# Moving one third of the adaLN product from TensorE matmuls to GpSimd, in a one-core Trainium2 decoder block

## The reference, cut to what matters

```python
mod = jnp.dot(jax.nn.silu(c), w_ada[l]) + b_ada[l]          # c: (1, 1024), w_ada: (1024, 6144)
sh1, sc1, g1, sh2, sc2, g2 = jnp.split(mod[:, None, :], 6, axis=-1)
h = rmsnorm(x, norm1_g[l]) * (1.0 + sc1) + sh1
x = x + g1 * token_mixer(h, w_in[l], ..., w_merge[l])       # projection, attention, conv, gates, merge
h = rmsnorm(x, norm2_g[l]) * (1.0 + sc2) + sh2
x = x + g2 * moe(h, ...)                                    # top 4 of 32 experts
return rmsnorm(x, normf_g)                                  # x: (1, 256, 1024), one layer
```

## Time and profile before

| | |
|---|---|
| median of 3 runs | 1197.81 us |
| the profiled execution: its time, its span | 1198.26 us, 1196.5 us |
| TensorE busy, share of the span | 1157.0 us, 97% |
| VectorE, ScalarE, GpSimd busy | 413.8 us, 208.8 us, 19.9 us |
| HBM read | 469.08 MB, 393 GB/s over the span |
| mean granted TensorE clock | 0.998 |

### The profile page before, as it was taken

How to read it: one execution, slowest core, us unless ns; L and a number is a source line. 1 busy time by engine, 2 the same in 40 slices (tenths; PEclk the granted TensorE clock), 3 DMA queues, 4 the chain that set the end, 5 groups by cost and what they waited for, 6 DMA issues and landing times.

```text
span 1196.5 us, 15173 instructions
## 1 busy us (share of the span) xinstructions
PE 1157.0 (97%) x6133; PEld 524.9 (44%) x6133; DVE 413.8 (35%) x792; ACT 208.8 (17%) x331; POOL 19.9 (2%) x38
## 2 busy tenths in 40 slices
PE   7999999999999999999999999999999999999997
PEld 4787899984333333333333333333333333333332
DVE  4667776663232322222222222222222322222222
ACT  4346644341011010101010101010101101010001
POOL 1000010000000000000000000000000000000000
PEclk9999999999999999999999999999999999999999
DMA  9998457699999999999999999999999999999995
GB/s 337 393 374 326 170 188 245 245 393 368 428 422 431 428 432 427 437 426 434 431 428 433 426 437 427 426 427 428 429 436 425 436 428 432 432 427 435 422 426 234
DMA packets 53171, 470.55 MB, mean 393 GB/s; under 512 B 4479, under 2 KB 10060, under 8 KB 31894
## 3 DMA queue, kind: packets, MB, share of 16 engines
q1 hardware_dynamic: 50884, 467.99, 94.1%
q10 hardware_dynamic: 2258, 2.16, 0.6%
HBM read 469.08 MB, written 1.06 MB: 393 GB/s over the span
## 4 chain that ended last, share of the span: by engine, by line
PE 71%; DMA 24%; ACT 2%; SPq 1%; DVE 1%; issue 1%; DVEq 0%; ACTq 0%
PE ps L1104 25%; DMA expert<-in_w_down 17%; PE ps L1114 15%; PE ps L875 14%; DMA expert<-in_w_gate_up 6%; PE ps L1080 4%; PE ps L1052 3%; PE ps L1033 2%; PE ps L819 1%; PE ps L1060 1%; ACT r_cu L1358 1%; DMA ada_first<-in_w_ada 1%; PE ps L732 1%; SPq L489 1%; PE ps L1096 1%
## 5 line engine op out<-in xcount | busy, mean ns | idle before, releaser
L1104 PE MATMUL ps<-expert,r_work 128*64 128x512 f32 x2048 | 454.5, 595 | 5.5 <-DMA expert<-in_w_gate_up 4.6
L1104 PEld LDWEIGHTS ps<-expert,r_work 128*64 128x64 f32 x2048 | 141.3, 137 | 293.1 <-issue 283.2
L1114 PE MATMUL ps<-expert,r_work 128*64 128x512 f32 x1024 | 228.7, 596 | 10.2 <-DMA expert<-in_w_down 10.1
L1371 ACT ACTIVATE r_v<-r_v 128x512 f32<-128x512 f32 x32 | 20.1, 630 | 734.5 <-DVE r_v L1836 734.5
L1836 DVE TENSOR_SCALAR r_v<-ps 128x512 f32<-128x512 f32 x32 | 22.1, 692 | 326.7 <-PE ps L1104 326.7
L1114 PEld LDWEIGHTS ps<-expert,r_work 128*64 128x64 f32 x1024 | 70.0, 137 | 145.7 <-issue 123.7
L1503 DVE TENSOR_TENSOR w_lo<-stage,w_hi 128x2048 fp32r<-128x2048 f32 x36 | 82.2, 2289 | 38.3 <-ACT w_hi L1227 38.3
L875 PE MATMUL ps<-x_hi,w_hi 128*128 128x256 f32 x304 | 87.3, 287 | 1.0 <-issue 0.9
L875 PE MATMUL ps<-x_lo,w_hi 128*128 128x256 f32 x304 | 86.0, 283 | 0.0
L875 PE MATMUL ps<-x_hi,w_lo 128*128 128x256 f32 x304 | 85.9, 283 | 0.0
L1227 ACT ACTIVATE w_hi<-stage 128x2048 fp32r<-128x2048 f32 x36 | 68.9, 1913 | 92.9 <-PE ps L875 63.7
(11 more groups left out here) (230 smaller groups left out, 893.2 us busy)
## 6 DMA issues: line engine op xcount, KB each, us to landing
expert<-in_w_gate_up SPq DMA_DIRECT2D x44, 4096.0 KB
expert<-in_w_down SPq DMA_DIRECT2D x61, 2048.0 KB, 18.0
expert<-in_w_gate_up SPq DMA_DIRECT2D x40, 2048.0 KB, 38.0
stage<-in_w_in SPq DMA_DIRECT2D x24, 1024.0 KB, 7.0
stage<-in_w_ada SPq DMA_DIRECT2D x16, 1024.0 KB, 8.5
expert<-in_w_down SPq DMA_DIRECT2D x5, 1024.0 KB, 37.3
ada_first<-in_w_ada SPq DMA_DIRECT2D x16, 256.0 KB, 6.5
ada_first<-in_w_ada SPq DMA_DIRECT2D x8, 512.0 KB, 11.5
```

The costliest lines, as they stand in the source:

```text
L1104: mm = pe.matmul(ps[CAP * g:CAP * g + CAP, j, :], xg[:, 2 * (k % 4) + k // 4, :], buf[:, col:col + 512], start=False, stop=(k == KD - 1))
L1114: mm = pe.matmul(ps[CAP * half:CAP * half + CAP, bank, :], turned[:, ch, CAP * g:CAP * g + CAP], buf[:, col:col + 512], start=(q == 0), st ...
```

## The change

The second third of `w_ada` is no longer multiplied on TensorE. GpSimd scales each chunk in place by silu(c) of its rows (TENSOR_SCALAR) and adds it to a sum (TENSOR_TENSOR) in `r_xn`, the space of the normalised x, which is free once x is turned; the first chunk is scaled straight into the sum. TensorE adds the partitions behind product 18. The chunks move two places back in the stream, alternate between the two buffers in the gates' space, and the load of expert slot 2, which overwrites `r_xn`, moves from behind w11 to behind w20 and waits for that sum.

```diff
-ADA_AT = {7 + k: ("ada", 1, k) for k in range(KD)}
+ADA_AT = {9 + k: ("ada", 1, k) for k in range(KD)}
...
-ADA_SUMMED = 23
+ADA_SUMMED = {1: 18, 2: 23}
+FEW_FROM = 7
...
-    if STREAM[_n][0] == "ada" and not _wide:
+    if STREAM[_n][0] == "ada" and STREAM[_n][1] == 1:
+        _b = STAGE + STREAM[_n][2] % 2
+    elif STREAM[_n][0] == "ada" and not _wide:
         _b = WIDE - 1
+    elif STREAM[_n][0] == "w" and STREAM[_n][1] >= FEW_FROM:
+        _b = min(range(STAGE), key=lambda b: _last.get(b, -1))
...
-EARLY = {11: 2, 28: 0, 33: 1}
+EARLY = {20: 2, 28: 0, 33: 1}
...
             elif what[0] == "ada":
-                eng.wait_ge(ada_used, KD * what[1] + what[2] + 1)
+                eng.wait_ge(ada_pool_added, what[2] + 1)
...
                 if early == 2:
-                    sp.wait_ge(x_turned, 1)
+                    sp.wait_ge(ada_used, KD + 1)
...
+            def ada_add(k):
+                wait_chunk(pool, ("ada", 1, k))
+                src = front_chunk(STREAM.index(("ada", 1, k)))[0][:, :]
+                if k == 0:
+                    pool.wait_ge(x_turned, 1)
+                    ins = nc.gpsimd.tensor_scalar(ada_acc[1], src, cs32[:, k, 0:1], None, ALU.mult)
+                else:
+                    own.done(nc.gpsimd.tensor_scalar(src, src, cs32[:, k, 0:1], None, ALU.mult))
+                    own.wait()
+                    pool.wait_ge(ada_pool_added, k)
+                    ins = nc.gpsimd.tensor_tensor(ada_acc[1], ada_acc[1], src, ALU.add)
+                ins.then_inc(ada_pool_added, 1)
+            pool.wait_ge(c_ready, 1)
             for h in range(H):
+                ada_add(h)
                 pool.wait_ge(osq_done, h + 1)
                 if h >= 1:
                     pool.wait_ge(o_ready, h)
                 root(ors, oss, VD).then_inc(r_o_ready, 1)
...
-            def ada_chunk(b, k):
...
+            def ada_sum(b):
+                pe.wait_ge(mod_ready, b + 2)
+                pe.wait_ge(ada_pool_added if b == 1 else ada_added, KD)
...
-                if n in ADA_AT and ADA_AT[n][1] == 1:
-                    ada_chunk(*ADA_AT[n][1:])
...
-                if n == ADA_SUMMED:
-                    ada_sum()
+                for b in (1, 2):
+                    if n == ADA_SUMMED[b]:
+                        ada_sum(b)
...
+                    if p == GA0:
+                        act.wait_ge(ada_pool_added, KD)
```

More of the change, by code:

```diff
@@ L256, in block_kernel @@
         csig = r_conv[:, 1552:1560]
-        ada_acc = r_gb[:, :]
+        ada_acc = {1: r_xn[:, :], 2: r_gb[:, :]}
         nfb = r_gb[:, 0:D]
@@ L334, in block_kernel @@
         piece_landed = [[sem(f"last_down{p}_piece{n}_landed") for n in range(len(LAST_PIECES[p]))] for p in range(2)]
[L336 removed]
+        ada_added, ada_pool_added = sem("ada_added"), sem("ada_pool_added")
         ada_used, up_used, down_used = sem("ada_used"), sem("up_used"), sem("down_used")
@@ L723, in lam_column @@
                 pe.matmul(ps[:, 7, 16:17], ones[0:1, :], lam_s[:, 4:5], start=True, stop=True).then_inc(lam_ready, 1)
-            def ada_chunk(b, k):
[L727 to L730, removed]
-                for g in range(4):
[L732 to L741, removed]
+            def ada_sum(b):
+                pe.wait_ge(mod_ready, b + 2)
+                pe.wait_ge(ada_pool_added if b == 1 else ada_added, KD)
+                for g in range(4):
+                    m = pe.matmul(ps[32 * g:32 * g + 32, 6, :], ones[:, 0:32], ada_acc[b][:, 512 * g:512 * g + 512],
                                   start=True, stop=True)
@@ L1439, in mod_rows @@
             def mod_rows(b):
-                v.wait_ge(ada_used, (2, 4, KD, 2 * KD, 2 * KD + 1)[b])
+                v.wait_ge(ada_used, (2, 4, KD, KD + 1, KD + 2)[b])
                 v.wait_ge(ada_b_landed if b < 2 else ada_h_landed, 32)
@@ L1450, in ada_add @@
                 if k == 0:
-                    ins = v.tensor_scalar(ada_acc, src, cs32[:, k, 0:1], None, ALU.mult)
+                    ins = v.tensor_scalar(ada_acc[2], src, cs32[:, k, 0:1], None, ALU.mult)
                 else:
                     v.wait_ge(ada_added, k)
-                    ins = v.scalar_tensor_tensor(out=ada_acc, in0=src, scalar=cs32[:, k, 0:1], in1=ada_acc,
+                    ins = v.scalar_tensor_tensor(out=ada_acc[2], in0=src, scalar=cs32[:, k, 0:1], in1=ada_acc[2],
                                                  op0=ALU.mult, op1=ALU.add)
@@ L1658, in split_next @@
                         split(n + 2)
[L1660 to L1663, removed]
+                for b in (1, 2):
+                    if n == ADA_SUMMED[b] + 1:
+                        mod_rows(b + 2)
                 ends = n == LAST_CHUNK[p]
```

## The result

| | before | after | forecast |
|---|---|---|---|
| median of the runs, us | 1198.27 | 1265.65 | 1228 (1202 to 1243) |
| ratio, 95% interval | | 1.0561 [1.0548, 1.0574] | |
| span of the profiled execution, us | 1196.5 | 1264.1 | |
| mean granted clock | 0.998 | 0.971 | |

The sign was right, the size was not: +67.4 us where +30 stood.

A forecast was written before the change was run, and what follows sets the result against it. TensorE's queue in the front, with the probabilities' chain close beneath, was taken to bound the kernel. Head 7's probabilities 23.7 later, the sum's 1.06 and 5.2 before product 21 make 30.0: 1228 us, range 1202 to 1243.

The forecast's parts named there:

- What bounds the kernel, and that the front's delay passes to the end: Before 290 us TensorE's queue binds, and what this front gains or loses reaches the end one for one.
- TensorE gives back 8.0 and pays 1.06: TensorE loses eight chunks of 1.00 us and gains one sum of four matmuls, 1.06 us.
- I take 1.9 for one input: GpSimd's TENSOR_SCALAR on 2048 columns, first half of each pair, was put at 1.9 us.
- The TENSOR_TENSOR, 3.7 taken: GpSimd's addition of 2048 columns, second half of each pair, was put at 3.7 us, making a pair 5.7.
- The shared door towards VectorE: In attention, a two-input SBUF instruction of VectorE stands still while GpSimd's runs: steps of 14.0 us instead of 9.2, chance 0.52.
- Its constant: The part of the forecast 14.0 us attention step that is not GpSimd's two lengths.
- Head 7's mark: The turn using the last head's probabilities would start at 171.4 us instead of 147.70, 23.7 later.
- The wait before product 21: w21's load, behind 3 MB, and its split end 18.3 us after product 18, so TensorE waits 5.2 us.
- Loads behind it have room again: After product 21's wait, later loads are not late, since each split has two products of lead.
- Up to a few us: Idle of 6 us in 14 may lower TensorE's clock, 0.998 before, costing up to a few us.
- no door: Rival: GpSimd does not hold VectorE in attention; loads bind, steps of 9.8 us, total 1204, chance 0.14.
- VectorE keeps the door: Rival: VectorE's queued L1539 and L1545 pass before GpSimd's second half; steps of 11.1 us, total 1212, chance 0.20.

The follow-up runs named there:

- e6: The changed kernel with chunk 0 a MEMSET, GpSimd's other 14 large instructions on 2 columns, and the two edits: 2125.90 us, with a longer experts' stage.
- e12: The changed kernel with GpSimd's seven TENSOR_SCALARs on 640 of 2048 columns and its TENSOR_TENSORs on 1640: 1224.58 us.
- e2: The changed kernel with GpSimd's TENSOR_SCALAR of each pair replaced by three MEMSETs and its TENSOR_TENSOR by two and a half: 1243.7 us.
- The two edits: On the changed kernel, chunk 4 of the last third goes to the other wide buffer and expert slot 2 stands behind split 24, not 20: 1249.86 us.
- e10: The changed kernel, whole, with the two edits to the last third's buffer and the expert slot's place: 1249.86 us.
- e7: The kernel before with one edit alone: expert slot 2 loads behind split 20 and waits for product 18: 1206.24 us.
- e8: The changed kernel, whole, with 8 or 9 idle matmuls into an unused bank ahead of six of TensorE's waits: 1263.41 us.
- e9: The changed kernel with GpSimd's seven TENSOR_SCALARs on 256 of 2048 columns and its TENSOR_TENSORs whole: 1228.01 us.
- e4: The changed kernel with each large GpSimd instruction of the seven pairs cut into eight of 256 columns, same result: 1272.21 us.
- e11: e9 with the two edits to the last third's buffer and the expert slot's place: 1213.37 us.

## Why the prediction was wrong, point by point

- **What bounds the kernel, and that the front's delay passes to the end: right.** +68.6 at the last third's sum, +67.6 at the end of the span.
- **TensorE gives back 8.0 and pays 1.06: right**, where nothing else moves: -6.8 in e6. The row for the sum reads 1.04.
- **"I take 1.9 for one input": the step that failed.** Measured 5.48. The figure came from the bias mask, another instruction; a MEMSET does take 1.82, a TENSOR_SCALAR does not. Two columns take 0.19 and 256 take 0.93, so the row of the root, which showed the very operation, did not speak of its price per column. The TENSOR_TENSOR, 3.7 taken, is 4.49: the Trainium skill's 4497 ns (GPSIMD Engine Reference, "Elementwise — side-by-side cycle accounting") was the better number, and the trace agrees with it. By the sum above the two lengths make 4.4 us more a step. The prediction's range varied the two-input half alone (1.9 to 6.9); the one-input half stood at 1.9 without a range.
- **The shared door towards VectorE: right in this kernel**, for both halves, with nearly the turns forecast. Its constant was 1.0 too long: 14.0 - 5.6 = 8.4 against 7.36. One L1539 and both L1545 were counted behind the second half; but both L1551 are out by 152.82, as it begins, and of the two L1557 the first ends with it and only the second stands behind it. Head 7's mark: +44.7 for 23.7, and this term carries 21 of the 37.7 us missed (1265.65 for 1228). Of the 21, 8.0 lie ahead of pair 2, where chunk 0's instruction holds L1547 for 5 us (forecast 1.2) and pair 1 takes 10.3; 9.2 lie in the four steps up to pair 6 (65.2 for 56), 3.9 behind it.
- **But not as a rule for any length.** A TENSOR_SCALAR of 640 columns, which does take the prediction's 1.9 us, hardly holds VectorE (e12): with the prediction's two lengths the total is 1224.6, near the forecast 1228, for other reasons. Whether 2048 columns in 1.9 us would have held, no run shows; a MEMSET of 2048 columns in 1.8 us does hold VectorE's TENSOR_SCALARs (e2). The Trainium skill (SBUF — State Buffer, "Who interferes with whom") has the lock for the whole instruction; 2048, 1280 and 1640 columns agree, 640 columns of TENSOR_SCALAR do not, and the measurement decides. Its statement that a two-input VectorE instruction meets only reads of GpSimd's is borne out by e2.
- **Between the mark and the sum nothing was forecast; it is 14.6.** The last third's chunk 4 loads into the buffer that pair 7 reads. GpSimd ends pair 7 at 207.40, the load lands at 212.45, and VectorE, in order, has this chunk ahead of the next `w_lo` and L1413: hence the wait of 9.7 at L938. The two edits give back 7.8 there; in e10 3.3 us of that wait are left. Of the rest, 2.7 go to the slower clock, 0.76 in 200 to 220 us, with 48 matmuls in 8.42 for 5.75 of before.
- **The wait before product 21: right to a tenth in its place, too low in its price.** Forecast E + 18.3 with E the end of product 18; measured 245.44 - 227.12 = 18.32. The waits sum to 4.8 (3.3 and 1.5; 5.2 forecast), and 2.9 more go to the 96 matmuls behind them (14.45 for 11.52). Alone it costs 8.0 (e7). "Loads behind it have room again" held.
- **"Up to a few us" for the clock: right at most in size.** In the steps of the attention it costs nothing that e8 could give back; behind the two waits that follow, the matmuls take 2.7 and 2.9 us longer. Behind the last third's sum everything is shifted and not longer, as forecast, within 1 us.

Rivals: "no door" is no rival for this kernel, but gives the step of e9 and e12; "VectorE keeps the door" was not seen with the pair at its full lengths. Taken together, the 37.7 us missed are, within 0.1, 21.0 ahead of the mark, 14.6 between mark and sum, 3.0 behind the sum, less 1.0 that comes back at the end.

## What to carry to other kernels

Take the price of a large instruction only from a row of the same operation on the same engine; where there is none, the range has to reach over the factor by which operations of that engine differ, here 1.8 to 5.5 us for 2048 columns. Work given to GpSimd beside a VectorE that feeds the critical chain must be charged to that chain, and not taken as hidden: here, with large instructions, step = rest + GpSimd's time. GpSimd's own queue and the ring of the loads are two further floors (16.1 in e4, 9.8 in e12), and the longest of the three sets the step. When a slow engine becomes a buffer's last reader, follow that buffer to its next load and to everything that an in-order engine keeps behind it.

## What the runs showed of the hardware

- GpSimd on 128 x 2048 fp32: MEMSET 1.82 us, TENSOR_SCALAR 5.4 to 5.5 with or without a column of operands, TENSOR_TENSOR 4.49. One input costs more than two. At 1280 columns the TENSOR_SCALAR takes 3.56, at 640 1.92, at 256 0.93.
- The hold on VectorE has a step between 640 and 1280 columns of TENSOR_SCALAR: 0.4 us of 1.92, but all of 3.56. No run here says why.
- Who gets its turn is decided within hundredths of a us: in e9 an L1557 that begins 0.03 us before GpSimd's TENSOR_TENSOR passes (0.48 us), in e11 the same instruction, the same 0.03 us ahead, is held (4.81).
- A MEMSET on GpSimd holds VectorE's TENSOR_SCALAR, even on 2 columns, and lets its two-input instructions pass.
- TensorE's granted clock went below full where it stood waiting: in the attention of the kernel after, 120 to 220 us, it reads 0.67 to 0.76, a mean of its two levels, 1.2 and 2.4 GHz. With idle matmuls in the waits it read 0.85 to 0.98, the steps stayed at 17.3 us, and the kernel's median was 2.2 us lower.
